# A hybrid decoder layer on eight cores: shifts through the weights as biases, w_in in five blocks, gated first loads, two more x buffers, and phase B's next tile prepared inside ff2

## What is computed

```
mod = silu(c) @ w_ada + b_ada              -> sh1, sc1, gt1, sh2, sc2, gt2 (1024 each)
h  = rmsnorm(x, g_mix) * (1 + sc1) + sh1
u, v, B, C, hin = split(h @ w_in)          512 columns each
v  = rmsnorm per head of 64 (gelu(v)) * g_v
a  = gelu(u) * (tril(w_s) @ v + b_s)       chunks of 128 tokens, 8 heads
b  = B * conv3(C * hin)                    causal, width 3, depthwise
x1 = x + gt1 * (concat(a, b) @ w_out)
h2 = rmsnorm(x1, g_ffn) * (1 + sc2) + sh2
x2 = x1 + gt2 * (square(relu(h2 @ w_ff1)) @ w_ff2)
y  = rmsnorm(x2, g_final)
```

## Time and profile before

| | us |
|---|---|
| median of 3 runs | 837.09 (835.37 to 837.78) |
| the profiled execution | 834.73 |
| its span, slowest core (core 5) | 833.2 |
| spans of the 8 cores | 824.8 to 833.2 |
| busy in the span: TensorE, VectorE, ScalarE, POOL | 730.0, 395.6, 241.4, 153.8 |

### The profile page before, as it was taken

The page is one execution under the profiler, slowest core; times in us unless marked ns, Lnnn a source line. Parts: engine busy times, 40 slices in busy tenths (PEclk is TensorE's granted clock), DMA queues, the critical chain, the costliest instruction groups (busy, mean ns, idle before and its releaser), DMA issues.

```text
span 833.2 us, 16779 instructions; the slowest of 8 cores (824.8 to 833.2 us)
## 1 busy us (share of the span) xinstructions
PE 730.0 (88%) x6097; PEld 506.5 (61%) x6097; DVE 395.6 (47%) x791; ACT 241.4 (29%) x533; POOL 153.8 (18%) x156
## 2 busy tenths in 40 slices
PE   1348798598889999769899999999999999999996
PEld 1335487466556767644486596485584784864854
...
GB/s 155 186 183 172 182 160 28 170 184 238 144 207 113 241 153 153 182 188 170 82 91 1 26 78 5 26 78 1 35 69 1 102 1 26 77 2 26 26 1 52
DMA packets 51304, 83.58 MB, mean 100 GB/s; under 512 B 2292, under 2 KB 35846, under 8 KB 51222
## 3 DMA queue, kind: packets, MB, share of 16 engines
...
## 4 chain that ended last, share of the span: by engine, by line
PE 68%; DMA 11%; DVE 8%; issue 6%; ACT 3%; POOL 2%; another core or an unknown queue 1%; DVEq 0%; SPq 0%; ACTq 0%; POOLq 0%
PE ps L285 61%; DMA arena<-w_ada 5%; DVE arena L293 4%; PE ps L803 3%; DVE arena L296 3%; ACT arena L290 3%; DMA mod_scr<-arena 2%; DMA arena<-x_scr 2%; DMA x_scr<-arena 2%; POOL arena L293 2%; PE ps L408 1%; DVE arena L443 1%; PE ps L679 1%; PE ps L506 1%
## 5 line engine op out<-in xcount | busy, mean ns | idle before, releaser
L285 PE MATMUL ps<-arena 128*128 128x256 bf16 (+1 forms) x4384 | 634.4, 306 | 34.0 <-ACT arena L290 19.7
L285 PEld LDWEIGHTS ps<-arena 128*128 128x128 bf16 x4384 | 429.8, 99 | 225.6 <-issue 42.0
L290 ACT ACTIVATE arena<-ps 128x256 f32<-128x256 f32 (+4 forms) x379 | 163.6, 447 | 264.3 <-PE ps L285 100.6
L293 POOL TENSOR_TENSOR arena<-arena 128x1 f32<-128x1 f32 (+3 forms) x100 | 115.4, 1160 | 656.3 <-DVE arena L368 496.6
L293 DVE TENSOR_TENSOR arena<-arena 128x256 bf16<-128x256 f32 (+7 forms) x383 | 193.7, 529 | 78.8 <-ACT arena L290 60.4
L293 DVE TENSOR_TENSOR arena<-ps,arena 128x512 f32<-128x512 f32 (+6 forms) x161 | 84.5, 534 | 240.0 <-PE ps L285 151.0
L290 ACT ACTIVATE arena<-arena 128x256 f32<-128x256 f32 (+4 forms) x101 | 77.4, 772 | 319.2 <-DVE arena L293 277.0
L296 DVE SCALAR_TENSOR_TENSOR arena<-arena 128x256 f32<-128x256 f32 (+3 forms) x118 | 95.2, 808 | 20.9 <-POOL arena L293 14.0
L368 DVE TENSOR_SCALAR arena<-arena 128x1 f32<-128x1 f32 x46 | 6.8, 152 | 62.8 <-ACT arena L290 62.8
L803 PE MATMUL ps<-arena 128*128 128x512 bf16 x128 | 30.0, 393 | 4.7 <-DMA arena<-w_ff 4.7
L408 PE MATMUL ps<-arena 128*128 128x128 bf16 x256 | 20.8, 235 | 12.5 <-DVE arena L293 10.1
...
## 6 DMA issues: line engine op xcount, KB each, us to landing
...
```

What stands on the lines that cost most here:

```text
L285: ins = e.matmul(out, lhsT=l, rhs=r, start=(i == 0), stop=(i == n - 1))
L290: S.op("act", lambda e: e.activation(out=out, in_=in_, func=func, **kw), reads=reads, writes=writes)
L293: S.op(eng, lambda e: e.tensor_tensor(out=out, in0=in0, in1=in1, op=op), reads=reads, writes=writes)
```

## The change

*Shifts.* sh1B and `n_shift` go. h is only scaled, and since (h + sh) @ w = h @ w + sh @ w, the product of the shift with each weight block is made once: `win_bias` for u, C, h and B (32 matmuls with 2 columns, the shift split into a high and a low bf16 part), added as a per-partition bias by the eviction on ScalarE (Copy becomes Identity) or VectorE; `v_bias` for v, as rows that a ninth matmul with a row of ones adds in every A_v. In phase B the sample's ff1 product carries two more columns, from which the ReLU's bias bF is made. *Buffers.* w_in is five blocks. X has six buffers, `xr` says which the reload takes; tile 0's conv has four Csb and acc; ada_row has its own tile `rowst`; phase A's small constants leave w_ff1's slot 7. *Loads.* Tile 1's x waits for quarter 0, tile 2's for quarter 1, g_v and w_s for block u, the sample's x for v. w_ff1 5 and 7 start before tile 3, 4 and 6 in the last tiles; w_ff2 0 and 1 inside tile 7, then 3, 4, 2. *Order.* Tile 0's conv runs as a whole, tiles 1 and 2 and the steady tiles use one `conv`; both n_mod open a tile. In phase B n_stats stand behind ff1, n_mod and n_tr between ff2's groups.

The diff, cut to its core (of the setup from `t0, t1, t2, t3` on, the order after is shown without the lines taken out; the order before stands in the kernel, L986 to 1051):

```diff
-    w_in_t, _, ff2_off = take("w_in", 8 * DIN, BF16)
-    w_in_v = w_in_t.rearrange("p (k n) -> p k n", k=8)
+    ff2_off = cur[0]
+    win_g = {nm: take("win_" + nm, 8 * 512, BF16) for nm in "uvBCh"}
+    w_in_g = {nm: t[0].rearrange("p (k n) -> p k n", k=8) for nm, t in win_g.items()}
+    win_b = {nm: t[1] for nm, t in win_g.items()}
...
-        t, b, _ = sw[i - 2]
-        st = view(sw[0][2], 320, F32)[0:8, (i - 2) * 64:(i - 2) * 64 + 128]
-        sb = [sw[i - 2][1], sw[i - 1][1]]
+        st, sb = rowst[0:8, :], [rowst_b]
...
+        stt(hb, xt, rs, g1B, ALU.mult, ALU.mult, [xb, g1B_b] + rs_b, [hbb])
+    def sh_split(i, dst3, dst_b, c0):
+        m, mb = modT[i]
+        S.op("dve", lambda e: e.tensor_copy(out=dst3[:, :, c0], in_=m[:, :, 16]), reads=[mb], writes=dst_b)
+        tt("dve", dst3[:, :, c0 + 1], m[:, :, 16], dst3[:, :, c0], ALU.subtract, [mb] + dst_b, dst_b)
...
+    def win_bias(nm):
+        bk, bkb = next_bank()
+        def fn(e):
+            ins = None
+            for c in range(4):
+                for k in range(8):
+                    ins = e.matmul(bk[:, c * 2:c * 2 + 2], lhsT=w_in_g[nm][:, k, c * 128:(c + 1) * 128], rhs=shT3[:, k, :],
+                                   start=(k == 0), stop=(k == 7))
+            return ins
+        S.op("pe", fn, reads=[shT_b, win_b[nm]], writes=[bkb])
+        o = BA_COL[nm]
+        S.op("dve", lambda e: e.tensor_reduce(out=bA[:, o:o + 4], in_=bk[:, 0:8].rearrange("p (c t) -> p c t", c=4), axis=AX.X, op=ALU.add),
+             reads=[bkb], writes=[bA_b[nm]])
+    def v_bias():
+        bk, bkb = next_bank()
+        S.op("pe", mm_group(bk[0:2, :], [(shT3[:, k, :], w_in_g["v"][:, k, :]) for k in range(8)]), reads=[shT_b, win_b["v"]], writes=[bkb])
+        S.op("dve", lambda e: e.tensor_copy(out=vbK[0:2, :], in_=bk[0:2, :]), reads=[bkb, vbK_b], writes=[vbK_b])
+        tt("dve", vlo[0:2, :], bk[0:2, :], vbK[0:2, :], ALU.subtract, [bkb, vbK_b], [vlo_b])
+        S.dma("sp", vbK[32:34, :], vlo[0:2, :], [vlo_b, vbK_b], [vbK_b], "vbK")
...
+        act(ut[:, c * TILE:(c + 1) * TILE], bk[:, 0:TILE], AF.Gelu_apprx_tanh, [bkb, bA_b["u"]], [ub], bias=bcol("u", c))
...
+                            + [(onesK[0:34, :], vbK[0:34, :])]),
...
-        act(ct, bkC[:, 0:T], AF.Copy, [bkCb], [cb])
+        act(ct, bkC[:, 0:T], AF.Identity, [bkCb, bA_b["C"]], [cb], bias=bcol("C", c))
...
-        tt("dve", zt[:, 2:2 + T], bkH[:, 0:T], ct, ALU.mult, [bkHb, cb], [zb_])
+        stt(zt[:, 2:2 + T], bkH[:, 0:T], bcol("h", c), ct, ALU.add, ALU.mult, [bkHb, cb, bA_b["h"]], [zb_])
...
-        xt, xb, _ = X[2 + j]
+        xt, xb, _ = X[tl["xr"] + j]
...
+            sh_split(3, hsT3, [hsT_b], 16)
...
+                    ins = e.matmul(bk[:, (f % 16) * 18:(f % 16 + 1) * 18], lhsT=ff1_v[f // 4][:, k, (f % 4) * 128:(f % 4 + 1) * 128],
...
+        act(rt, bk[:, 0:TILE], AF.Relu, [bkb, bF_b[f // 16]], [rb], bias=bF[:, f:f + 1])
...
+    def B_next(nxt, step):
+        if nxt is None:
+            return
+        if step < 2:
+            n_mod(nxt, step)
+        else:
+            n_tr(nxt, 0)
+            n_tr(nxt, 1)
...
+                if (j, n) != (1, 1):
+                    B_next(nxt, 2 * j + n)
...
+        for np_, p in enumerate((0, 1, 3, 4, 2, 5, 6, 7)):
...
+            if 4 <= np_ < 7:
+                B_next(nxt, np_ - 4)
...
+        n_load(tA[1], j, after=[ff1_b[ADA_SLOT[0]]])
...
+        n_load(tA[2], j, after=[ff1_b[ADA_SLOT[1]]])
+    load(gvB, g_v.partition_broadcast(128), [gvB_b], "gvB", after=[win_b["u"]])
+    load(wst3, w_s.rearrange("h t s -> t h s"), wst_b, "wst")
+    load(xS, x_s.rearrange("t (k n) -> (t k) n", k=8), [xS_b], "xS", after=[win_b["v"]])
+    load(scS, sconv.rearrange("t (j n) -> (t j) n", j=8), [scS_b], "scS")
+    for j in range(2):
+        n_mod(tA[1], j)
...
     t0, t1, t2, t3 = tA[0:4]
+    setup_spatial()
+    win_bias("u")
     for c in range(4):
         A_u(t0, c)
     for j in range(2):
         n_tr(t1, j)
     for c in range(4):
         A_u(t1, c)
+    S.op("pool", lambda e: e.affine_select(out=wst3, in_=wst3, compare_op=ALU.is_ge, fill=0.0, base=0,
+                                           pattern=[[0, 8], [-1, 128]], channel_multiplier=1), reads=wst_b, writes=wst_b)
+    v_bias()
     for j in range(2):
         n_stats(t2, j)
     for j in range(2):
+        n_mod(t2, j)
+    for j in range(2):
         A_v(t0, j)
+    for j in range(2):
+        n_tr(t2, j)
+    for j in range(2):
+        n_load(t3, j)
+        n_load(tA[4], j)
     setup_spatial_pe()
     for j in range(2):
         A_vn(t0, j)
     for j in range(2):
         A_v(t1, j)
     for j in range(2):
         A_spatial(t0, j)
     for j in range(2):
         A_vn(t1, j)
     for c in range(4):
         A_u(t2, c)
     for j in range(2):
+        A_v(t2, j)
+    for j in range(2):
         A_spatial(t1, j)
     for j in range(2):
         A_vn(t2, j)
+    win_bias("C")
+    win_bias("h")
+    for c in range(4):
+        A_ch(t0, c)
+    win_bias("B")
     for j in range(2):
         A_spatial(t2, j)
+    for c in range(4):
+        A_b(t0, c)
+    setup_sample()
+    def conv(tl, at_0=None, at_1=None, at_2=None, at_3=None):
+        def do(fs):
+            for f in fs or ():
+                f()
+        do(at_0)
+        A_hist(tl)
+        A_ch(tl, 0)
+        A_ch(tl, 1)
+        A_b(tl, 0)
+        do(at_1)
+        A_ch(tl, 2)
+        A_b(tl, 1)
+        do(at_2)
+        A_ch(tl, 3)
+        A_b(tl, 2)
+        do(at_3)
+        A_b(tl, 3)
+    conv(t1, None, [lambda: n_stats(t3, 0)], [lambda: n_stats(t3, 1)], None)
+    conv(t2, [lambda: n_mod(t3, 0), lambda: n_mod(t3, 1), lambda: ada_cols(4), lambda: ada_dma(8)],
+         [lambda: n_tr(t3, 0), lambda: n_stats(tA[4], 0)], [lambda: n_tr(t3, 1), lambda: n_stats(tA[4], 1)],
+         [lambda: ada_cols(5), lambda: ada_dma(9)])
+    ff1_dma(7)
+    ff1_dma(5)
...
     def steady(i, mid, end, nxt, nn):
         tl = tA[i]
+        for j in range(2):
+            n_mod(nxt, j)
+        for j in range(2):
+            A_v(tl, j)
         if mid is not None:
             reload(mid)
-        n_mod(nxt, 0)
-        for j in range(2):
-            A_v(tl, j)
-        n_mod(nxt, 1)
-        ex()
         for j in range(2):
             if nn is not None:
                 n_load(nn, j)
+        ex()
         for c in range(4):
             A_u(tl, c)
         for j in range(2):
             A_vn(tl, j)
+        if end is not None:
+            reload(end)
+        if i == NT - 1:
+            for p, nm in ((0, "u"), (1, "v")):
+                alias_after([ff2_b[p]], [win_b[nm]])
+                ff2_dma(p)
         ex()
         if mid is not None:
             wout(mid)
         ex()
-        n_tr(nxt, 0)
-        A_hist(tl, 0)
-        A_ch(tl, 0)
-        A_ch(tl, 1)
-        A_b(tl, 0)
-        n_tr(nxt, 1)
-        A_hist(tl, 2)
-        A_ch(tl, 2)
-        A_b(tl, 1)
-        if end is not None:
-            reload(end)
-        ex()
-        A_ch(tl, 3)
-        if nn is not None:
-            n_stats(nn, 0)
-        A_b(tl, 2)
-        for j in range(2):
-            A_spatial(tl, j)
-        A_b(tl, 3)
+        conv(tl, [lambda: n_tr(nxt, 0)], [lambda: n_tr(nxt, 1), ex],
+             [(lambda: n_stats(nn, 0)) if nn is not None else ex],
+             [lambda: A_spatial(tl, 0), lambda: A_spatial(tl, 1)])
...
+        lambda: ff1_dma(4),
...
+        lambda: (s_mod(x1sT, x1sT_b, 4, 3), ff1_dma(6)),
+        lambda: s_ff1(0),
+        lambda: (s_ff1(1), alias_after([f1Ts_b], [xsT_b, zhist_b]), s_relu(0)),
...
-    bcast_load(3, sh1B, sh1B_b)
...
-    ff1_dma(6)
-    ff1_dma(7)
-    alias_after(ff2_b[0:5], list(win_b.values()))
-    for p in range(5):
+    for p, nm in ((3, "C"), (4, "h"), (2, "B")):
+        alias_after([ff2_b[p]], [win_b[nm]])
...
-    s_jobs = {(1, 3): lambda: s_ff1(0), (1, 7): lambda: s_ff1(1), (1, 11): lambda: s_ff1(2), (1, 15): lambda: (s_ff1(3), s_relu()),
-              (2, 3): lambda: s_ff2(0), (2, 7): lambda: s_ff2(1), (2, 11): lambda: s_ff2(2), (2, 15): lambda: (s_ff2(3), s_fin1()),
-              (2, 20): lambda: s_rs(), (2, 25): lambda: s_fin2(), (2, 29): lambda: s_fin3()}
+    s_jobs = {(0, 9): lambda: s_ff1(2), (0, 13): lambda: (s_ff1(3), s_relu(1)),
+              (1, 3): lambda: s_ff2(0), (1, 8): lambda: s_ff2(1), (1, 13): lambda: s_ff2(2), (1, 18): lambda: (s_ff2(3), s_fin1()),
+              (1, 23): lambda: s_rs(), (1, 29): lambda: s_fin2(), (2, 5): lambda: s_fin3()}
     for i, tl in enumerate(tB):
         nxt = tB[i + 1] if i + 1 < NT else None
         for f in range(4 if i == 0 else 0, 32):
-            if nxt is not None:
-                if f == 4:
-                    n_load(nxt, 0)
-                    n_load(nxt, 1)
-                if f in (12, 15):
-                    n_stats(nxt, (f - 12) // 3)
-                if f in (18, 22):
-                    n_mod(nxt, (f - 18) // 4)
+            if nxt is not None and f == 4:
+                n_load(nxt, 0)
```

(14 more changed lines are left out.)

276 lines of the change are left out of this document (114 added, 162 removed).

## The result

The changed kernel takes **868.65 us** (median of 4, 867.13 to 870.02) beside 836.23 (834.35 to 837.78) for the kernel before: ratio 1.0388, 95% interval 1.0357 to 1.0419. It is slower by 3.9%; 803 us and "faster" were forecast. The profiled execution took 869.43, its span 867.8.

A forecast was written before the change was run, and what follows sets the result against it. TensorE sets the end almost everywhere, with time to be had in its holes. Startup -5.0, steady tiles -11.9-2.7-4.2+3.2, passage -18.9 and phase B +5.3 sum to -34.2: profiled 834.73 becomes 800.5, the median 803, range 788 to 817.

The forecast's parts named there:

- First loads: Startup: x of tiles 1 and 2 waits for quarters 0 and 1; block u whole at 52.3 instead of 60.0, -7.7 us.
- the 5.6 us of the v bias: Startup: uncovered TensorE wait for the 2 KB DMA before A_v(t0), priced from a 4 KB row write; part of +10.2.
- Rival A: Startup: the v bias's 2 KB DMA takes 17.5 us instead of 5.6, giving 815; sign: v wait over 10; chance 0.15.
- Rival C: More waits go than counted: the other half of VectorE's and no v wait, giving 793 us; chance 0.09.
- rival E: Whole kernel: nothing of weight gained, TensorE's holes move instead of closing; chance 0.02.
- the price of 4.5 us per MB: Startup: cost of SyncE loads beside weight loads, from 6.7 us extra over two intervals for 1.5 MB.
- Startup: Up to 139.17 us: loads -7.7, column biases +3.5, v bias +10.2, job order -9.8, transpose waits -3.1, v rows +1.9.
- Steady tiles: After startup: 10.06 us hole and restart -11.9, wait at 210.68 -2.7, VectorE waits -4.2, ten v rows +3.2.
- The passage: From phase A to B: wait for ScalarE -12.2, low clock -2.0, waits for w_ff2 -4.7; -18.9 in all.
- Rival B: Passage stays bound by its loads: w_ff2 cannot begin before 318, loads end at 400, giving 813 us; chance 0.12.
- Phase B: Transposes leave the seam between ff1 and ff2; tiles 1 to 6 each lose 0.89 us, +5.3.
- rival D: C eviction's Identity needs another activation table, two loads per A_ch: 885 us if all shows; chance 0.04.

The follow-up runs named there:

- e1: Changed kernel with tile 2's x loads issued before w_ada quarters 4 to 7 are asked for: 820.12 us, ratio 0.9797 to the kernel before.
- e9: Kernel before with only tile 2's x loads moved behind the eighth w_ada quarter's request and gated on the second quarter's slot: 896.83 us, ratio 1.0669.
- e10: Changed kernel with the v bias's small DMA issued on ScalarE's queue instead of SyncE's: 872.53 us, ratio 1.0378 to the kernel before.
- e7: e1 with phase B's g1B broadcast loaded earlier, inside tile 6: 815.58 us, ratio 0.973 to the kernel before.
- e6: e1 with phase B's old seam for tiles 2 to 7 (statistics and scaling in ff1, transposes between ff1 and ff2): 817.31 us, ratio 0.9739.
- e5: e1 with the v bias's low part made by a second group of eight products, without the small DMA: 819.4 us, ratio 0.9746.
- e3: Kernel before with only ada_row copying into its own tile instead of the sample's scratch: 828.39 us, ratio 0.9905.
- e4: Kernel before with tile 1's statistics behind tile 0's ff1, its scaling and transposes between ff2 pieces, weight loads unchanged: 837.84 us, ratio 1.0021.
- e2: Changed kernel with tile 2's x loads gated on w_ada quarter 6 instead of quarter 7: 867.5 us, ratio 1.0362 to the kernel before.

## Why the prediction was wrong

**The step that failed** is in *First loads*: "t1's x now waits for quarter 0, t2's for quarter 1". The first half is right; in the second the gate was read by the name in its brackets, and not by the last writer of that slot at that line. The text then priced quarter 1's arrival and charged nothing for SyncE's queue behind it. Had it been followed (tile 2's x, g_v, w_s, x_s, sconv, then the small DMAs), the 5.6 us of the v bias would have read "5.6 behind the arrival of the eighth quarter". e1 and e9 show it from both sides: without it -48.5 us in the changed kernel, with it alone +56 in the old one. Rival A had the place and the victim, but by the DMA's own slowness, which e1 and e10 refute: asked for in time it takes 8.0 and 7.1 us of waiting (7.5 in e7). e6's 11.1 is over the 10 that the prediction named as A's sign, but the DMA's part of it is 9.6, not 17.5, and far from the 58.5. None of the rivals had a queue held up. Rival C fell too: VectorE's waits did not go, they moved, as rival E had it for all of TensorE's holes.

The kernel before has a gate misread in the same way: L881 names `ADA_SLOT[3]`, which is quarter 3 (slot 1), and not quarter 1, as the description of that kernel has it. Its trace shows tile 1's x issued just as quarter 3 lands (its column job runs at 22.57):

```profile
22.49 0.90 SPq L99 DMA_DIRECT2D arena<-x_p  x2
```

So that load fell into the first of the two intervals priced and w_s into the second, and the price of 4.5 us per MB is a mean of two unlike intervals: 2.7 us longer with 1 MB of x, 4.0 longer with 0.5 MB of w_s. Block u came in e1 1.4 us earlier than the text had it.

**With the fault out,** by the steps and e1:
- *Startup,* -5.0 forecast, -3.5 measured. Block u's first product was put at 52.3 and came at 50.9. The wait in front of the v products was put at 6.7 (VectorE 1.1, the DMA 5.6) and measured 8.03 in e1: about 1.5 until VectorE's subtraction ends at 67.26, and 6.5 for the DMA behind it. The same DMA takes 5.6 in e10, 6.0 in e7 and 9.6 in e6. The 18 products took 7.12 us where 18 later ones take 4.37: a restart of 2.8, not 1.8. But e5 shows that its price was not the wait: what hides under it is the mask of w_s, which the text had as "inside the wait already counted". That was right, and meant that 7 of these us were not the v bias's to give back. Beside the 5.6 the text put the rule of the Trainium skill ("DMA: Bandwidth & Descriptors", Queues, rings and completion order) that completion waits for an engine's earlier writes; the 5.6 to 9.6 us agree with "cannot come quickly" and don't test it further.
- *Steady tiles,* -15.6 forecast, -2.2 measured: the second wrong step, and the larger one of the kernel without the fault. TensorE's idle time in the stage fell from 19.5 to 12.6 us (ten and seven entries of the timelines), where 17.0 and a restart had been taken off. The 10.06 became 1.94 (-8.1 where -11.9 stands); e3 shows that in the old order the scratch tile held only 5.8 of it. The 2.67 is gone, but a stall of 3.06 of the kind called issue, of which the kernel before has none, stands near its place, in the sample's products. Of VectorE's waits 1.53 stays as 1.48, and two new ones of 2.31 and 2.17 come in tile 7 from "it delays them by one scaling ... 0", which was priced without g1B's broadcast; e7 removes the first and most of the second. The v rows were put at 0.32 each: e1's 50 products with two v rows among them take 11.20 to the next start, the 48 before took 10.37, so 0.42 each, 4.2 for ten and not 3.2. The windows show the clock below full in e1 at 200 to 210 (0.71) and 310 to 320 (0.83), as before at 150 to 170 (0.53, 0.79), where e1 has 1.00: the low clock moved, it did not go. In sum the forecast was too good by 3.8 in the 10.06 us hole, by 3.1 at the 2.67, by 5.0 in VectorE's other waits (5.5 before, 6.3 in e1, where 4.2 were taken off) and by 1.0 in the v rows.
- *The passage,* -18.9 forecast, -19.3 measured. No wait for w_ff, none of ScalarE for x_scr, and ff2 of tile 0 ends at 393.0. e4 shows that the order without the loads gives nothing. Rival B is refuted.
- *Phase B,* +5.3 forecast, +8.5 measured: 0.98 a tile, from 57.11 to 58.09, in place of 0.89, with 1.47 idle at ff2's start where 1.3 to 1.4 were named, and at the start of tile 1 a loss not foreseen: the wait for tile 0's evictions is 2.24, before 0.83, and 40 products then run at a low clock, 6.10 us where the same 40 take 4.53. It comes with the new order of tile 0's ff2 and not with s_ff1's move: e4, with s_ff1 where it was, waits 2.18 at the same place (at 415.71, before the fourth group of tile 1).
- *Table loads:* two, as taken; rival D is refuted (the Trainium skill's "ScalarE: Activation LUTs", Table sets, had it so).

So two errors of different kinds: one line read wrongly, 48.5 us, that turned the sign; and the steady term, 13.4 us too good, because holes were given whole to the wait that the trace named as their last, and VectorE's waits were taken to go where they moved. In the passage the hit is earned, as the named waits went; in the startup it is in part luck, as block u came 1.4 us early and offset part of a v wait and restart that cost 2.3 us more than their terms.

What stays open: the stalls called issue, 1.3 to 4.1 us in the sample's products of the steady tiles and up to 3.4 in phase B's first ff1, in the changed kernel and all that are built on it, together 5.0 us in e1; and why an issue takes 4.5 us in e2.
